# A mixture of 32 experts: gather 32 places for each expert, run four experts in the column quarters of TensorE, use weights as they land

## The reference

```python
def hier_moe(h, router_grp, router_grp_b, router_exp, router_exp_b, w_gate, w_up, w_down):
    '''Two-level routing: top-1 expert group, then top-2 experts inside that group; SwiGLU experts.'''
    t = h.reshape(-1, shape[-1])                                  # 256 x 1024
    grp_p = softmax(t @ router_grp + router_grp_b)                # 4 groups
    p_grp, g_sel = lax.top_k(grp_p, 1)
    in_grp = ...                                                  # the 8 expert logits of that group
    top_logit, top_idx = lax.top_k(in_grp, TOP_K)                 # TOP_K = 2
    w_exp = one_hot(top_idx) weighted by softmax(top_logit) * p_grp
    for grp in range(N_GROUPS):                                   # 4 groups of 8 experts, D_EXPERT = 256
        hid = silu(t @ w_gate[grp]) * (t @ w_up[grp])
        out = out + (hid * combine[:, grp, :, None]) @ w_down[grp]

h_lat = h_lat + m_lat[5] * hier_moe(modulate(rmsnorm(h_lat, norm_ffn_g), m_lat[3], m_lat[4]), ...)
return rmsnorm(h_lat, final_norm_g)
```

## Time and profile before

| what | before |
|---|---|
| time, median of 3 runs | 2503.92 us (2502.22 to 2505.46) |
| profiled execution: span from first to last instruction | 2506.8 us |
| TensorE matmul busy | 97% |
| VectorE, ScalarE busy | 56%, 48% |
| DMA traffic | 396 MB, mean 158 GB/s |

### The profile page before, as it was taken

How to read it: one execution, slowest core, us unless ns; L and a number is a source line. 1 busy time by engine, 2 the same in 40 slices (tenths; PEclk the granted TensorE clock), 3 DMA queues, 4 the chain that set the end, 5 groups by cost and what they waited for, 6 DMA issues and landing times.

```text
span 2506.8 us, 52399 instructions
## 1 busy us (share of the span) xinstructions
PE 2421.1 (97%) x23215; PEld 2091.8 (83%) x23215; DVE 1408.6 (56%) x2208; ACT 1193.3 (48%) x1725; POOL 296.2 (12%) x417
## 2 busy tenths in 40 slices
PE   7999999999999999999999999899999888999998
PEld 7999888799999998878899995686477777878887
DVE  5655544366646655543666567454434454378886
ACT  5434465444344444474454346431255342277775
POOL 0100000031101100000301000462133222000000
PEclk9999999999999999999999999999999989999999
DMA  8754522266656755422457522201201111479995
GB/s 262 243 205 152 205 92 92 105 202 216 223 183 202 236 185 179 146 97 106 143 193 236 213 77 101 70 3 40 68 35 37 33 42 46 131 246 365 368 364 181
DMA packets 269445, 396.15 MB, mean 158 GB/s; under 512 B 9624, under 2 KB 173133, under 8 KB 269085
## 3 DMA queue, kind: packets, MB, share of 16 engines
q1 hardware_dynamic: 267481, 389.32, 45.6%
q0 software_dynamic: 1120, 2.17, 0.3%
q10 hardware_dynamic: 612, 1.24, 0.1%
HBM read 391.66 MB, written 1.05 MB: 157 GB/s over the span
## 4 chain that ended last, share of the span: by engine, by line
PE 82%; DVE 6%; DMA 5%; ACT 3%; issue 2%; SPq 1%; POOL 0%; ACTq 0%; DVEq 0%
PE ps L284 81%; DMA RB<-in_moe_w_up 5%; DVE gwl L449 2%; ACT gwh L440 1%; SPq L521 1%; PE ps L1151 0%; SPq L416 0%; DVE wl L449 0%; DVE AR L659 0%; ACT wh L440 0%; ACT AR L2903 0%; DVE AR L1972 0%; PE ps L543 0%; ACT AR L2895 0%; ACT AT L1205 0%
## 5 line engine op out<-in xcount | busy, mean ns | idle before, releaser
L449 DVE TENSOR_TENSOR wl<-RB,wh 128x2048 fp32r<-128x2048 f32 (+5 forms) x189 | 412.2, 2185 | 281.1 <-ACT wh L440 280.6
L284 PE MATMUL ps<-H,RB 128*128 128x256 f32 (+2 forms) x1728 | 451.7, 420 | 2.8 <-ACT AR L2874 1.3
L440 ACT ACTIVATE wh<-RB 128x2048 fp32r<-128x2048 f32 (+5 forms) x189 | 342.2, 1814 | 227.4 <-PE ps L284 200.0
L284 PEld LDWEIGHTS ps<-H,RB 128*128 128x128 f32 (+1 forms) x1728 | 320.2, 189 | 113.7 <-issue 75.6
L284 PE MATMUL ps<-xhf,wl 128*128 128x256 f32 x1408 | 402.4, 286 | 2.4 <-DVE xlf L688 2.4
L284 PE MATMUL ps<-xlf,wh 128*128 128x256 f32 x1408 | 398.9, 283 | 0.0
L284 PE MATMUL ps<-xhf,wh 128*128 128x256 f32 x1408 | 398.8, 283 | 0.0
L284 PE MATMUL ps<-AR 64*64 64x64 f32 (+3 forms) x8296 | 264.6, 236 | 39.9 <-issue 24.7
L284 PEld LDWEIGHTS ps<-AR 64*64 64x64 f32 (+2 forms) x8296 | 231.4, 142 | 79.1 <-issue 64.2
L284 PEld LDWEIGHTS ps<-xhf,wl 128*128 128x128 f32 x1408 | 270.6, 192 | 13.2 <-issue 9.4
L284 PEld LDWEIGHTS ps<-xlf,wh 128*128 128x128 f32 x1408 | 270.8, 192 | 0.1
(11 more groups left out here) (445 smaller groups left out, 4108.1 us busy)
## 6 DMA issues: line engine op xcount, KB each, us to landing
RB<-in_ffn_w_gu SPq DMA_DIRECT2D x88, 1024.0 KB, 7.7
RB<-in_w_in SPq DMA_DIRECT2D x23, 2048.0 KB, 7.8
RB<-in_ffn_w_down SPq DMA_DIRECT2D x16, 2048.0 KB, 7.8
RB<-in_w_gate SPq DMA_DIRECT2D x16, 2048.0 KB, 8.9
RB<-in_moe_w_gate SPq DMA_DIRECT2D x32, 1024.0 KB, 7.6
RB<-in_moe_w_up SPq DMA_DIRECT2D x32, 1024.0 KB, 10.2
RB<-in_moe_w_down SPq DMA_DIRECT2D x32, 1024.0 KB, 8.2
RB<-in_ada_w SPq DMA_DIRECT2D x12, 2048.0 KB, 9.9
```

Of the source, the lines that this page charges most:

```text
L284: return M.matmul(o, lhsT, rhs, start=start, stop=stop, skip_group_check=True)
L440: S.activation(self.pair(h)[0], of(slot_of(*key)), ACT.Copy).then_inc(*did("high", *mark))
L449: V.tensor_tensor(lo, of(slot_of(*key)), hi.bitcast(F32), ALU.subtract).then_inc(*did("low", *mark))
```

## The change

Each expert gets 32 places. Four experts make a round n (8 rounds). `CHOSEN` is 256 positions by 8 rounds x 128 places (4 experts x 32). The rank of a position is counted within its expert, so the second choice within the group must be known before the rank matmuls; the flag asks for at most 32 positions for each expert. The stationary of a product is 32 columns wide and works in its column quarter; the weights are the moving side, in float32 from the slot itself, so the splitting on ScalarE and VectorE and the low parts are gone. The channel order is changed so that a partition holds 8 consecutive channels (`own` makes shift and scale in that order with two small products): gate and up then come in runs of 8 KB. Down comes in runs of 4 KB for half of four experts. Six more 2 MiB slots lie in memory that the scan and `merge` leave, and the second `out2` job goes behind three expert jobs in SP's list. The sums of all rounds stay in four PSUM banks that begin with the residual itself (`rows_pe`: rows of `XT` by products with the identity), so the result is in rows, and the final norm has no transposes.

```diff
 def fill_e(e):
-                v = slot.rearrange("p (k g n) -> p k g n", k=KD, g=2)
-                return [(v[:, :, s, :], rows(A[n][0, e // 8, e % 8]))
+                v = slot.rearrange("p (s n) -> p s n", s=2)
+                return [(v[:, s, :], A[n][0, e // 8, e % 8].rearrange("(p k) n -> p (k n)", k=KD))
...
+        slots = [RB[:, i, :] for i in range(NSLOT)] + [sb(f"EX{i}", STAGE + c, [4096]) for i, c in enumerate(
+            (13568, 17664, 21760, 9472, 4736))] + [sb("EX5", O_H, [4096])]
+        opened = {3: [("rw_out", 7, 1)], 4: [("rw_out", 7, 1)], 5: [("rw_out", 7, 1)], 6: [("turned", "ya", 1)],
+                  7: [("summed", 7)], 8: [("mgate", 1, 7), ("glo", 1)]}
+        expert_slots = (3, 4, 5, 8, 6, ring_jobs[0] % NSLOT, (ring_jobs[0] + 1) % NSLOT, (ring_jobs[0] + 2) % NSLOT, 7)
...
+            of_experts = [(kind, n, x) for n in range(8) for kind, x in
+                          (("e", 0), ("e", 1), ("e", 2), ("e", 3), ("d", 0), ("d", 1))]
+            for i, (kind, n, x) in enumerate(of_experts):
+                if i == 3:
+                    job_no[("out2", 1)] = len(jobs)
+                    jobs.append(out2_last)
+                slot = expert_slots[i % len(expert_slots)]
...
@@ merge @@
+                PE.wait_ge(*at("own_in"))
+                for k in range(KD):
+                    ins = mm(ps[0:16, 16 * k:16 * k + 16], ident.rearrange("p (q k) -> p k q", k=KD)[:, k, :], OWN_IN,
+                             True, True)
...
+                mm(ps[:, 0:128], RST[0:16, 128:256], RST[0:16, 0:128], True, True).then_inc(*did("own"))
@@ Route @@
+            def rows_pe(self):
+                for c in (0, 4):
+                    for t in LAT:
+                        ps = bank(("acc", t, c // 4), among=(4, 5, 6, 7))
+                        for j in range(4):
+                            ins = mm(ps[:, 128 * j:128 * j + 128], XT[:, c + j, 128 * t:128 * t + 128], ident, j == 0, False)
...
@@ gathered, on TensorE @@
+                def gather(n):
+                    for half in range(2):
+                        for k in range(4 * half, 4 * half + 4):
+                            for t in LAT:
+                                ins = mm(ps[:, 128 * (k % 4):128 * (k % 4) + 128], UT[:, t, k, :], CHOSEN[:, t, n], t == 0, t == 1)
+                def up(n):
+                    for k in range(KD):
+                        for c in range(4):
+                            PE.wait_ge(*landed("e", 4 * n + c))
+                            ins = mm(ps[32 * c:32 * c + 32, :].rearrange("p (s n) -> p s n", s=2),
+                                     XG[n % 2][:, k, 32 * c:32 * c + 32], up_of(4 * n + c)[:, :, k, :], k == 0, k == KD - 1)
+                def down(n):
+                    for half in range(2):
+                        PE.wait_ge(*landed("d", n, half))
+                        for o in range(2):
+                            for c in range(4):
+                                ins = mm(ps[o][32 * c:32 * c + 32, :], HT[n % 2][:, half, 32 * c:32 * c + 32],
+                                         w[:, c, 512 * o:512 * o + 512], half == 0, half == 1)
+                def spread(n):
+                    for t in LAT:
+                        for o in range(2):
+                            ins = mm(accs[2 * t + o], BACK[n % 2][:, 128 * t:128 * t + 128], Y[:, 512 * o:512 * o + 512],
+                                     False, n == 7)
+                gather(0); up(0); (combine weights); gather(1); (m5_rows)
+                for n in range(8):
+                    if n:
+                        up(n)
+                        if n < 7:
+                            gather(n + 1)
+                    back(n); turned(n); down(n); spread(n)
```

More of the change, by code:

```diff
@@ L298, in everyone, with job @@
                     x.wait_ge(*at(*mark))
-        jobs, job_no = [], {}
-        def job(key, fill, free):
+        jobs, job_no, ring_jobs = [], {}, [0]
+        def job(key, fill, free, slot=None):
             job_no[key] = len(jobs)
-            jobs.append((fill, free))
+            if slot is None:
+                slot = ring_jobs[0] % NSLOT
+                ring_jobs[0] += 1
+            jobs.append((fill, free, slot))
         def fill_gu(w, c):
@@ L3121, in tensor @@
                 route.pe(KD - 1)
+                route.rows_pe()
             def scalar():
@@ L3204, in moe_jobs @@
             del jobs[first_expert:]
[L3205 to L3213, removed]
-                if kind == "e":
[L3215 to L3220, removed]
-                else:
[L3222 to L3228, removed]
@@ L3459, in places_dve @@
                     *did("combined"))
-                for k in range(3, KD):
-                    low_x(k)
-                    if k == 4:
-                        self.ws_g.low(3)
         def experts(route):
@@ L3468, in experts @@
             route.places_dve()
-            area, rank, cmb = route.area, route.rank, route.cmb
             for x in (PE, DV, AC, PO, SP):
@@ L3472, in experts @@
             fits = nc.values_load(route.FLAG[0:1, 0:1], min_val=0, max_val=1)
-            here = ([dict(x.seen) for x in (PE, DV, AC, PO, SP)], dict(counts.n), dict(bank_at), list(bank_free), sent[0])
+            here = ([dict(x.seen) for x in (PE, DV, AC, PO, SP)], dict(counts.n), dict(bank_at), list(bank_free), sent[0],
+                    dict(holder))
             with nc.If(fits > 0):
                 load_ring(len(jobs))
-                gathered(area, route)
+                gathered(route)
             for x, seen in zip((PE, DV, AC, PO, SP), here[0]):
@@ L3483, in experts @@
             sent[0] = here[4]
+            holder.clear()
+            holder.update(here[5])
             moe_jobs("d")
@@ L3690, in scalar @@
[L3690 to L3705 removed]
+                PV = OWN.rearrange("p (k s) -> p k s", s=2)
@@ new lines, in scalar @@
+                AC.wait_ge(*at("owned"))
+                for k in range(KD):
+                    AC.wait_ge(*at("xd", k))
+                    S.activation(XM[:, k, :], ps_of("xd", k)[:, 0:T], ACT.Identity, bias=PV[:, k, 1:2],
+                                 scale=PV[:, k, 0:1]).then_inc(*did("xd_out", k))
+                for j, (n, c, i) in enumerate(order):
+                    AC.wait_ge(*at("dg", 4 * n + c))
+                    if j > 1:
+                        AC.wait_ge(*at("c_scaled", *order[j - 2]))
+                    S.activation(S1[:, j % 2, :], ps_of("up", "d", n, c, i)[:, 0:T], ACT.Silu).then_inc(
+                        *did("d_silu", n, c, i))
@@ L3741, in vector @@
                 end.dve()
-            everyone(("xm_low", 7), ("low", "g", 2), ("xm", 7), ("expert_exp",), ("combined",))
+            everyone(("acc",), ("expert_exp",), ("combined",), ("chosen", 1, 2))
             tensor()
```

603 lines of the change are left out of this document (289 added, 314 removed).

## The result

The changed kernel takes **2415.62 us** (median of 4 runs, 2413.30 to 2420.29), against 2503.07 us for the kernel before, timed beside it: ratio 0.9654 (95% interval 0.964 to 0.9669), 87 us less. The forecast was 2422 (2405 to 2451). A second timing, on another occasion, gave 2419.68 us and 0.9681 (0.9666 to 0.9695).

What follows compares the result with a forecast made beforehand. The prediction took the expert stage to be bound by its loads, TensorE 5% behind. Faster loads (36 us), head start (35) and tail (11) took 82 us off the 2506.8 us span: 2425, median 2422 us, range 2405 to 2451.

Steps and rivals of the forecast that it cites:

- Part 1, the rate: Expert loads: 422 GB/s for gate and up, 410 for down; a round of four experts 30.1 us instead of 34.5.
- The rival at 364 GB/s: Expert loads stay at the stage's old rate; 39 jobs take 224.7 us, 29 more, giving 2451 us; chance 0.12.
- Part 2, TensorE in a round: Four experts' TensorE work sums to 22 us, hidden under 30.1 us of loads; `up` 7.2 us with quarters side by side.
- Part 3, the head: Start of expert stage: nine expert jobs go before the branch; job 10 waits for `up(0)`, until 2210.5 us (2205.5 to 2216.5).
- Part 4, the end: After the last loads: last expert lands at 2398, span ends at 2425 us; tail 12 us instead of 23.
- The sum: Whole kernel: span 2425 us instead of 2506.8, 82 us less; median 2422 us, taken 2.9 us below the span.
- The three items in which the gain was told: Split of the 82 us: faster loads 36, five more jobs in early and a sooner gapless start 35, tail 11.
- taking work from TensorE alone would give almost nothing: Expert stage before the change: bound by loads, 17.26 us for two experts, with TensorE 5% behind at 16.4 us.

Runs made afterwards that it cites:

- runs_1k: Changed kernel with gate and up interleaved by channel in the slot, so their loads come in 1 KB runs instead of 8 KB; 2440.38 us.
- six_slots: Changed kernel with six buffers for experts instead of nine; 2447.75 us, ratio 0.9773 to the kernel before.
- warm_end: Changed kernel with five unread products of constants ahead of the last expert's products in the last `up`; 2420.58 us, ratio 0.9671 to the kernel before.

## Why the prediction held, step by step

**Part 1, the rate: right.** 418 GB/s was the mean of the sum, 417 is measured over 151 us; 348, 409 and 418 for the three run lengths against 349, 410 and 422. The short stretches of the earlier trace rows told the long-run rate. The rival at 364 GB/s (2451) has its picture in `runs_1k`, which loads at 364 in the window above and at 368 over 195 us, and takes 2440 us: its price, 29 us, stands against 28.5 in the stage and 25 or 21 in the medians.

The Trainium skill (DMA: Bandwidth & Descriptors, "Where 436 GB/s comes from") would have the loads at about 358 GB/s, and this case's 417 over five rounds does not agree. The same page's section "Measured (HBM→SBUF, 128 partitions, SWDGE, issued from GpSimd)" reports 425 GB/s for 16 MB on one core with its neighbour idle, and keeps 358 for two cores that load at once. One core runs here, and 417 stands near that figure. The prediction had drawn only on the first of the two.

**Part 2, TensorE in a round: right.** `up` 7.07 us at full clock (7.2), `down` 3.64 (3.6), gather 3.8 (4.9), `spread` 3.68 (3.5); 76% busy against "about 70%", the difference being `up` at half clock (9.1 to 9.9 us in the middle rounds), which the loads hide. ScalarE and VectorE are as idle as stated.

**Part 3, the head: the mechanism right, the time 12.6 us too late, and outside its bounds.** Nine jobs were issued by 2178, as said, and the tenth waited for `up(0)`, at 2197.90 instead of 2210.5 (bounds 2205.5 to 2216.5). 6.9 us of it are the scan, which ran at a better clock. The other 5.7 are terms of this part: `own` added 1.2 and not 2; from the route's last matmul to the flag it took 7.6 and not 8.1; from the flag to the end of `up(0)` 11.6 us passed and not 16, since branch and activations took less, and the gather ran at full clock (3.83 instead of the 6 taken from a window with the clock at 0.67). That last term was not wrong by nature: in six_slots and warm_end the same gather takes 5.5 and 5.4 us. One term was forgotten: the rows now go to SBUF with the channels permuted, and the four activations take 3.88 us instead of 2.42.

From the tenth issue to the last landing (2397) it took 199 us, predicted 197.8.

**Part 4, the end: right within 3 us.** From the last expert's landing to the end of the span 23.7 us instead of 27: `up(7)` 8.54 (8.7 with half of the clock's price), 1.9 (2.5), 3.6 (3.6), then 5.8 to the last scale (7) and 3.7 behind it (5 kept).

**The sum.** Span 2411.5 against 2425, 13.5 less: -6.9 scan, -5.7 head, +2.4 to the last expert's landing, -3.3 end. The median is only 6.4 us below the forecast: the profiled execution is the fastest of four, and its span lies 4.1 us under the median, where the forecast had taken it 2.9 us above. The scan's 6.9 us belong to that execution; without them 6.6 us are left, which is about what the medians show. That it isn't 9 is luck, since the 2.4 us go the other way. The three items in which the gain was told (36 rate, 35 head start, 11 end) stand as an account of this profile, but not as what the edits are worth singly: undone one at a time, the rate costs 25 us, the jobs ahead 19, the turns between quarters 77; and done alone the rate brings 3. What the prediction called "taking work from TensorE alone would give almost nothing" is borne out in mid-stage by `runs_1k` (34.3 us for four experts, 34.3 before). That the rate alone would give almost nothing either follows from the same rows, TensorE busy 40.00 of 40 us, and wasn't said; there the prediction had TensorE 5% behind, and it was 2%.

## What to carry to other kernels

Where two resources are within a few per cent of each other (2% here), price the edits as a set: each alone buys the distance to the other, here 3 of the 25 us. Loads in long runs pay once nothing else is full: 348, 409 and 418 GB/s at 1, 4 and 8 KB. Products for the column quarters should alternate between quarters, one after the next, in the order in which they are issued. Work between waits that seems free to move may be what keeps TensorE's clock for what follows it: the ranks took 1.20 us behind the rows and 2.34 behind a wait. And when two profiles of nearly the same kernel are compared, take off first what the clock did in the part that was not changed, here up to 4 us.

## What the runs showed of the hardware

- Four quarters run side by side with moving sides in four different buffers: 7.07 us for 64 records of 512 columns, 0.11 each. Without alternation TensorE overlaps only some four records at a change of quarter (12.25 us in pairs, 22.5 singly).
- While TensorE waited for loads in each round (1.92 of 5 us busy), its granted clock went to 0.55, which is the 1.2 GHz level; the first records of `up` then last 1.06 us instead of 0.59, and `up` 8.5 to 9.9 us instead of 7.1.
- ScalarE's write of 128 x 512 from PSUM with the channels permuted took 1.13 us an instruction, against 0.69 for the same instruction in the kernel before, which writes the channels in their order (in groups of instructions with shapes apart, first after, then before):

```profile
L3344 ACT ACTIVATE AR<-ps,AR 128x512 f32<-128x512 f32 x4 | 3.9, 1129 | 0.2 <-DVE AR L3371 0.2
```

```profile
L3344 ACT ACTIVATE AR<-ps,AR 128x512 f32<-128x512 f32 x4 | 2.4, 687 | 0.2 <-DVE AR L3379 0.2
```
